# First scan chunk loaded by the projection's program, and four row blocks of the output projection taken in the scan's program, in a two-layer SSD, mLSTM and differential-attention kernel

## The reference, cut to what matters

```
h = _f32(_rmsnorm(x, ab_norm_g[i]))
proj = h @ _f32(ab_w_in[i])
z_a, xbc, dt_raw, z_b, q, k, v, ig, fg, og = jnp.split(proj, AB_SPLITS, axis=-1)
y_a = _ssd(xbc, dt_raw, z_a, ...)      # conv, silu, recurrence, gate by silu(z), rms, norm_g
y_b = _mlstm(q, k, v, ig, fg, og, z_b, ...)
y = jnp.concatenate([y_a, y_b], axis=-1) @ _f32(ab_w_out[i])
...
h = _f32(_rmsnorm(x, c_norm_g[i]))
proj = h @ _f32(c_w_in[i])
y_c = _diff_attn(q, k, v, z, ...)
y = y_c @ _f32(c_w_out[i])
x = x + y.astype(x.dtype)              # at the end of both layers
return _rmsnorm(x, final_norm_g)
```

## Time and profile before

| | us |
|---|---|
| median of 3 runs | 1641.59 |
| lowest and highest | 1641.34, 1643.62 |
| the profiled execution | 1643.99 |
| its span in the trace | 1642.3 |
| PE busy in the span | 1553.0 (95%) |
| DVE, ACT, POOL busy | 900.2, 649.3, 581.9 |
| mean granted PE clock | 0.975 |

### The profile page before, as it was taken

How to read it: one execution, slowest core, us unless ns; L and a number is a source line. 1 busy time by engine, 2 the same in 40 slices (tenths; PEclk the granted TensorE clock), 3 DMA queues, 4 the chain that set the end, 5 groups by cost and what they waited for, 6 DMA issues and landing times.

```text
span 1642.3 us, 23740 instructions
## 1 busy us (share of the span) xinstructions
PE 1553.0 (95%) x9153; PEld 1331.8 (81%) x9153; DVE 900.2 (55%) x1466; ACT 649.3 (40%) x1272; POOL 581.9 (35%) x333
## 2 busy tenths in 40 slices
PE   6899999999999979998799999989999999999797
PEld 5688989898999958777588878878888887877686
DVE  5765879584854348888344344335444334563633
ACT  5443433353532124443344342325554323555421
POOL 4334354444344335656464530142121122121111
PEclk8999999999999979999799999999999999999999
DMA  4124243332333155555475440021111011103622
GB/s 157 50 78 131 78 129 103 103 116 90 116 116 106 67 176 193 180 165 180 158 280 193 142 126 14 26 84 52 46 35 63 33 36 53 61 27 122 227 81 103
DMA packets 149756, 176.36 MB, mean 107 GB/s; under 512 B 8590, under 2 KB 125458, under 8 KB 148626
## 3 DMA queue, kind: packets, MB, share of 16 engines
q1 hardware_dynamic: 149650, 174.91, 32.1%
HBM read 122.46 MB, written 52.43 MB: 106 GB/s over the span
## 4 chain that ended last, share of the span: by engine, by line
PE 44%; DVE 2%; POOL 2%; DMA 1%; issue 1%; ACT 1%; SPq 0%; POOLq 0%; DVEq 0%; ACTq 0%
PE a_ps L2195 20%; PE a_ps L2240 4%; PE a_ps L2215 4%; PE a_ps L2146 3%; PE a_ps L2148 3%; PE a_ps L2147 3%; PE a_ps L2227 2%; PE a_ps L2307 2%; PE a_ps L2309 2%; PE a_ps L2308 2%; POOL a_w_lo L1713 1%; DVE b_y_T L1984 1%; DMA b_w_raw<-in_c_w_in 1%; PE a_ps L2248 0%; PE a_ps L2163 0%
## 5 line engine op out<-in xcount | busy, mean ns | idle before, releaser
L1713 POOL TENSOR_TENSOR a_w_lo<-b_w_raw,a_w_hi 128x1024 fp32r<-128x1024 f32 x72 | 172.0, 2391 | 375.6 <-DVE a_w_hi L1973 252.9
L352 POOL TENSOR_TENSOR p_w_lo<-b_y_T,p_w_hi 128x1024 fp32r<-128x1024 f32 x60 | 154.7, 2581 | 215.2 <-ACT p_w_hi L411 215.2
L2195 PE MATMUL a_ps<-a_h_hi,a_w_hi 128*128 128x512 f32 x384 | 162.5, 423 | 2.9 <-DVE a_h_lo L1951 2.9
L2195 PE MATMUL a_ps<-a_h_lo,a_w_hi 128*128 128x512 f32 x384 | 152.3, 397 | 0.0
L2195 PE MATMUL a_ps<-a_h_hi,a_w_lo 128*128 128x512 f32 x384 | 152.3, 396 | 0.0
L841 PE MATMUL p_bank<-p_w_hi,p_hi_s 128*128 128x256 f32 x512 | 145.0, 283 | 0.0
L841 PE MATMUL p_bank<-p_w_lo,p_hi_s 128*128 128x256 f32 x512 | 144.9, 283 | 0.0
L841 PE MATMUL p_bank<-p_w_hi,p_lo_s 128*128 128x256 f32 x512 | 144.9, 283 | 0.0
L645 DVE SCALAR_TENSOR_TENSOR b_w_raw<-p_out_raw,p_cols,b_w_raw 128x1024 f32<-128x1024 f32 x60 | 122.1, 2041 | 13.0 <-ACT b_w_raw L442 11.6
L841 PE MATMUL p_bank<-p_w_hi,p_hi 128*128 128x256 f32 x384 | 108.9, 283 | 0.0
L841 PE MATMUL p_bank<-p_w_lo,p_hi 128*128 128x256 f32 x384 | 108.7, 283 | 0.0
(11 more groups left out here) (378 smaller groups left out, 3939.4 us busy)
## 6 DMA issues: line engine op xcount, KB each, us to landing
b_y_T<-in_ab_w_in SPq DMA_DIRECT2D x33, 512.0 KB, 4.2
tok<-p_out_raw SPq DMA_DIRECT2D x64, 256.0 KB, 2.4
b_w_raw<-in_ab_w_out SPq DMA_DIRECT2D x32, 512.0 KB, 3.7
b_w_raw<-in_c_w_in SPq DMA_DIRECT2D x32, 512.0 KB, 4.0
c_gz<-tok SPq DMA_DIRECT2D x8, 1536.0 KB, 10.4
feat<-b_w_raw SPq DMA_DIRECT2D x20, 512.0 KB, 2.9
c_fe<-feat SPq DMA_DIRECT2D x8, 1280.0 KB, 6.8
yt<-b_y_T SPq DMA_DIRECT2D x8, 1024.0 KB, 11.0
```

The costliest lines, as they stand in the source:

```text
L352: gp.tensor_tensor(w_lo[s % SLOTS][:, :, :], operand(n, split_of(n, p))[:, :, :], w_hi[s % SLOTS][:, :, :].bitcast(F32), ALU.subtract).the ...
L1713: gp.tensor_tensor(w_lo[:, w, :], w_raw[u % W_RAW][:, :], w_hi[:, w, :].bitcast(F32), ALU.subtract).then_inc(S["l_wlo"], 1)
L2195: mm = pe.matmul(o, x, y, start=(k == 0 and q == 0), stop=(k == KT - 1 and q == 2))
```

## The change

**At the first boundary.** The last two blocks of the projection's SP list now load most of the scan's first chunk, into buffers that all programs share: 16 of its 20 feature rows into `w_raw` (in block 11), its first gate into `y_T[0]`, the four key rows and the small constants into `y_raw` (in block 12), and the two other gates into `y_T[1]` (behind two of the last stores). SP no longer waits at the end for the stores; that wait is now the first thing in the scan's program, for SP (ahead of the first chunk's values and of chunk 1) and for POOL (ahead of one memset). PE takes the features' transposes of chunk 0 ahead of the first decays, and waits for masks and columns later.

**At the second boundary.** The weights' ring (`w`), the first six `y` pieces (`yy`) and all PSUM banks (`ps`) are now shared, and the program of the scan loads, casts and splits units 0 to 5 and multiplies units 0 to 3 of the mid products. For row tiles 1 to 3, units 0 and 1 stand between the last chunk's state and its transposes, unit 2 between the two halves of those transposes, and unit 3 behind them; row tile 0 of all four comes last. ACT, POOL and DVE do the splits in the last chunk's list, at places named `spare`. One clean-up is left between the two programs instead of three. In `layer2`, PE starts at unit 4; the 1024 gains `cols`, before loaded as 8 rows of 128 and transposed by PE, are loaded by one DMA of single elements.

```diff
@@ projection_ab, SP
+                if n == nb - 2:
+                    for s in (0, 1):
+                        sp.wait_ge(S[f"c_stored{s}"], 16 * 2 * nf)
+                    load_first["features"](sp)
+                if n == nb - 1:
+                    sp.wait_ge(S["l_wlo"], seq(n, "7") + 1)
+                    for r in (0, 2):
+                        sp.wait_ge(S[f"t_stored{r}"], 16 * (nt - 2))
+                    load_first["gate_a"](sp)
+                    sp.wait_ge(S["l_wlo"], seq(n, "5") + 1)
+                    load_first["keys"](sp)
                 if kinds[n] == "t":
                     for i, k in ((1, 1), (1, 0), (0, 1)):
                         store_tokens(n, i, k)
-            for s in (0, 1):
-                sp.wait_ge(S[f"c_stored{s}"], 16 * 2 * nf)
-            for r in range(8):
-                sp.wait_ge(S[f"t_stored{r}"], 16 * nt)
+                        if n == nb - 1 and (i, k) == (1, 1):
+                            sp.wait_ge(S["l_wlo"], STEPS)
+                            load_first["gates_b"](sp)
@@ scan_chunks, SP
-            load_consts(sp)
-            for n in (0, 1):
-                load_chunk(sp, chunk, feat, tok, n, n)
+            for r in ahead["t_stored"]:
+                sp.wait_ge(r, 16 * TOK_BLOCKS)
+            load_values(sp, chunk, tok, 0, 0)
+            load_chunk(sp, chunk, feat, tok, 1, 1)
...
             store_y(TILES - 2, 0)
-            store_y(TILES - 1, 1)
+            for u in range(W_RAW, UNITS_RING + W_RAW):
+                sp.wait_ge(S["l_wlo"], u - W_RAW + 1)
+                load_ahead_w(sp, ahead, w_mid, u)
+                sp.wait_ge(S["d_ylo"], u - 1)
+                load_ahead_y(sp, ahead, yt, u)
+                if u == UNITS_RING - 1:
+                    store_y(TILES - 1, 1)
@@ scan_chunks, PE
             outputs(TILES - 1, 1, (TILES - 1) // 2)
+
+            pe.wait_ge(S["d_cmem"], 4 * TILES)
+            for u in (0, 1):
+                mid_products(u, (2, 3, 1))
             pe.wait_ge(S["d_y"], 2 * TILES)
             turn(TILES - 1, 0)
+            mid_products(2, (2, 3, 1))
             turn(TILES - 1, 1)
+            mid_products(3, (2, 3, 1))
+            pe.wait_ge(S["d_yT"], 4 * TILES)
+            for u in range(MID_EARLY):
+                mid_products(u, (0,)).then_inc(S["p_w"], 1)
@@ scan_chunks, ACT
             over(act, 0, TILES - 1, body)
+            act.wait_ge(S["d_yb"], TILES - 1)
+            high_pieces(0)
+            high_pieces(1)
             memory_squares(TILES - 1)
+            high_pieces(2)
             ssd_squares(TILES - 1)
             ssd_norm(TILES - 1)
+            for u in range(3, UNITS_RING):
+                high_pieces(u)
@@ scan_chunks, DVE (low_y: y_lo = y_raw - y_hi, 128x512)
-            outputs(TILES - 1, 1, (TILES - 1) // 2)
+            outputs(TILES - 1, 1, (TILES - 1) // 2, spare=low_y)
+            low_y(2)
             ssd_means(TILES - 1)
             turn(TILES - 1, 0, 1, (TILES - 1) // 2)
+            low_y(3)
             turn(TILES - 1, 1, 1)
+            for u in range(4, UNITS_RING):
+                low_y(u)
@@ layer2, SP
-                sp.dma_start(row_in[0:KT, :], norm_g).then_inc(S["rows_in"], 16)
+                sp.dma_start(cols[:, :], norm_g.rearrange("k p -> p k")).then_inc(S["cols_in"], 16)
@@ hybrid
-            first.enter_context(nc.cleanup_on_exit())
...
-                ctx.enter_context(nc.cleanup_on_exit())
```

More of the change, by code:

```diff
@@ L47 @@
 FEAT_T = XBC_T + QK_T
+TOK_BLOCKS = 8
 AB_OUT_T = (SSD_INNER + ML_INNER) // P
@@ L1578, in layer2 @@
         S = {n: m.sem(n) for n in names}
[L1579 removed]
+        S |= ahead["mid"]
         TOGETHER = 3
```

302 lines of the change are left out of this document (181 added, 121 removed).

## The result

| | before | changed |
|---|---|---|
| median of 12 runs, us | 1642.92 | 1630.92 |
| lowest and highest | 1635.04, 1645.16 | 1627.64, 1633.29 |
| profiled execution | 1643.99 | 1628.21 |
| its span | 1642.3 | 1626.5 |
| mean granted PE clock | 0.975 | 0.981 |

The ratio is 0.9923, with a 95% interval of 0.9914 to 0.9933: the changed kernel is 0.8% faster. The forecast was 1619.4 us, in a range of 1613.5 to 1626.5; the time lies above that range. The 12 times of the changed kernel fall in two groups, six from 1627.6 to 1629.0 and six from 1632.8 to 1633.3. The profiled execution belongs to the lower one.

The account below looks back on a forecast made before the run. PE bounds the kernel, busy 1553.0 of 1642.3 us (95%), so gains come from its idle stretches at two program boundaries. First 8.9 us plus second 13.3 gives 22.2: 1641.6 - 22.2 = 1619.4 us, range 1613.5 to 1626.5.

Parts of the forecast that it names:

- First boundary, the program's start: Projection to scan: without SP's wait the scan's program starts at 578.1, before at 579.92; the early loads cost nothing.
- First boundary, up to the outputs: Scan's start to the first product of the outputs: outputs start at 589.6 or 592.4, 591.2 taken; A = 8.9 us.
- from there the work is that of before, 7.76 us: From the third quarter of decays to the outputs: same work as before, about 7.1 us at full clock.
- the sum: Both boundaries together: A + B = 22.2 us gained, giving 1619.4 us.
- Second boundary, the matmuls: Scan's end to the mid products' end: 23.9 us of early work without pause, one clean-up of 1.5, 16.6 us gained.
- The single elements: Last program's load of 1024 single elements: taken as 0, with 3 us in the range for a late unit 7.
- The rival that was to make the kernel slower: Last program: slow issue of the single elements delays the loads behind it; some 27 us eat up the gain; chance 0.02.
- it does not do what it says: Rival at the first boundary: outputs wait for values, or PE's program starts later; 1622 to 1624 us, chance 0.07.
- Second boundary, are the splits ready: Last chunk of the scan: POOL about even, DVE delayed by collisions with POOL; 2.5 us lost, between 0 and 5.6.
- What is not covered is DVE: Last chunk: two `low_y` on DVE stand still beside POOL operations of 2.4 us, ahead of `s_den` and `s_cmem`.
- the upper end of 5.6: Last chunk: largest loss, in us, if POOL goes first at both `low_y`.
- The median and the profile: Whole kernel: profiled execution 1621.8 us, median 2.4 us below it, so 1619.4.

Follow-up runs that it names:

- experiment 3: Changed kernel with the first chunk's and constants' loads issued in the scan's program again: 1639.14 us with keys first, 1636.76 us in the old order.
- experiment 5: Kernel before, profiled again: 1643.82 us; with the projection's splits in two large buffers: 1642.43; also with one PSUM tensor and `out_raw` moved: 1643.65.
- experiment 6: Changed kernel with last-chunk splits kept apart: 1622.56 us; plus useless PE matmuls 1618.49, or later memsets 1619.5, or later memsets with fillers 1619.47 and 1619.17.
- experiment 1: Changed kernel with POOL's first low part of the last chunk behind the `s_state` decay: 1623.42 us; with DVE's first `low_y` moved instead: 1629.01; unaltered: 1630.16.

## Why the prediction was wrong

**First boundary, the program's start: right.** SP no longer waits, PE starts 2.27 us behind the start of DVE's last operation (2.75 by the forecast), and no early load is late. That the projection would end as before was taken for granted; in the changed kernels it ends 2.8 us later, 1.6 us in this pair of profiles. The loads are not to blame (experiment 3); the time lies in 384 matmuls that each take some 7 ns longer, and the cause of that is open (experiment 5).

**First boundary, up to the outputs: one term wrong, one not seen.** 15.05 us were needed where 12.9 were forecast, and 15.7 to 16.0 in the second clock pattern. The step that failed is "from there the work is that of before, 7.76 us, at full it is about 7.1". It took 9.08 us (585.40 to 594.48), with 0.58 of the clock from 586 to 594. Before, the half clock from 579.5 to 593.5 had lain over 6 us of PE standing still, and of the work behind it all but the first 1.7 us ran at full. With the waits gone the work itself moved into the low stretch. Where the clock was 1.00 there (the two kernels of experiment 6 with later memsets and no filler inside the scan), the same work took 7.03 us (584.00 to 591.03) and 7.04 us, as the sum has it for the full clock: its size was right, and its clock was wrong. Pricing the moved operations at the clock that they had before was the mistake: work that moves towards a boundary moves into the boundary's clock. The other term was not seen at all: with the constants early, DVE's tables run beside POOL's memsets and last 2 us (experiment 6); before, they ran at 583.1 to 583.4, behind the memsets. In the profile after, PE did not wait for them; in the five of the second pattern it stopped 0.96 to 0.98 us.

**Second boundary, the matmuls: right.** 23.9 us of early products without a pause, one stop of 1.25 us (1.5 forecast) and the mid products 181.4 us behind the last state product, where 182.4 were forecast. The single elements cost nothing: that load took 0.38 us to issue, and PE did not wait at unit 7. The rival that was to make the kernel slower is out, and so is that it does not do what it says.

**Second boundary, are the splits ready: the mechanism right, the term mis-sized.** "What is not covered is DVE" was right, and that two inputs in SBUF stand still beside POOL too. The sum priced two `low_y` at 1.3 us more each. The first took 1.47 us (0.8 more) and the second 0.69. What it left out is that POOL's newly placed operation, and the one right behind it, meet DVE's next operations as well, however small: `s_den`, 3.6 us more, and then the half clock behind PE's stop: the 32 small matmuls took 6.06 us where experiment 1 had 3.76, and the row behind them 1.0 us more. 2.5 us forecast became 7.4, more than the upper end of 5.6. Experiment 1 shows it: with POOL's operation alone moved, the median is 6.7 us lower and this stretch 5.6 us shorter. The Trainium skill ("SBUF — State Buffer", "Who interferes with whom") names this for a DVE instruction with two SBUF inputs against a POOL instruction that reads SBUF, and says that not the shape but the order decides who waits. By that rule the trace agrees: a 128x4 operation waited as long as a 128x512 one.

**The median and the profile.** The forecast took over from before that the median is 2.4 us below the profiled execution; in the changed kernel it is 2.7 us above. That moved the result by 5.1 us, nearly as much as all of the account's misses (5.9). 1.3 us of it are the 3 runs by which the median before was taken; the rest fits the changed kernel's two groups, of which the profile caught the lower. A kernel whose executions fall in two groups has no fixed distance between its profile and its median.

## What to carry to other kernels

When an operation is put into an idle place of POOL or DVE, list all operations of the other of the two that run in its time, with their inputs, and price each at a whole wait, also the ones of a few columns; a chain of small dependent operations is the worst neighbour. When waits at a program's start are removed, price the work that moves up at the clock of that stretch, not at the clock it had, and look at what now runs beside what. Move splits forward only with enough matmuls above them: without these the kernel was 23 us slower here, and slower than the kernel before.

## What the runs showed of the hardware

- A DVE `TENSOR_SCALAR` with one input and its output in SBUF stood still beside POOL memsets, which read nothing: 2.04 and 1.95 us beside them, 0.27 and 0.18 us when they came later. The same for `s_rms`, 128x4, beside POOL's low parts in experiment 1: 2.02 us instead of 0.16, up to their end at 772.96. A copy from PSUM (0.15 us) and a reciprocal (0.18 us) did not wait beside one.
- No single stop explains the granted clock at the scan's start, and neither does the sum of the stops. With stops of 1.10, 0.97 and 0.78 us it fell to half from about 585 to 599. With 1.10, 0.79 and 1.92 us it stayed at 1.00. With 1.11 and 1.92 us it stayed at 1.00 in one kernel and fell from about 593 to 596.5 in another. What else decides it was not found.
- Clearing one part's semaphores and meeting again stopped PE for 1.25 us where all else was ready, 1.24 to 1.56 us in the other kernels with the early products.
